# Matrix memory of a hybrid encoder layer: row maxima, sample keys, state decay and score order rewritten, unused products added

## The reference, cut to what matters

```python
def _mlstm_chunk(carry, inp):
    c_mat, n_vec, m_sc = carry
    q, k, v, ig, lf = inp
    b = jnp.cumsum(lf, axis=-1)
    d_log = jnp.where(causal, b[..., :, None] - b[..., None, :] + ig[..., None, :], -jnp.inf)
    g_log = b + m_sc[..., None]
    m_tok = jnp.maximum(g_log, jnp.max(d_log, axis=-1))
    w_intra = jnp.exp(d_log - m_tok[..., None]) * jnp.einsum('bhjd,bhsd->bhjs', q, k)
    inter = jnp.exp(g_log - m_tok)
    num = (inter[..., None] * jnp.einsum('bhvk,bhjk->bhjv', c_mat, q)
           + jnp.einsum('bhjs,bhsv->bhjv', w_intra, v))
    den = inter * jnp.einsum('bhk,bhjk->bhj', n_vec, q) + jnp.sum(w_intra, axis=-1)
    h = num / jnp.maximum(jnp.abs(den), jnp.exp(-m_tok))[..., None]
    m_new = m_tok[..., -1]
    w_state = jnp.exp(b[..., -1:] - b + ig - m_new[..., None])
    decay = jnp.exp(b[..., -1] + m_sc - m_new)
    c_new = decay[..., None, None] * c_mat + jnp.einsum('bhs,bhsv,bhsk->bhvk', w_state, v, k)
    n_new = decay[..., None] * n_vec + jnp.einsum('bhs,bhsk->bhk', w_state, k)
```

## Time and profile before

| | |
|---|---|
| median of 3 runs | 2208.29 us (2206.0 to 2211.57) |
| the profiled execution's own time | 2209.34 us |
| its span (first to last instruction) | 2207.5 us |
| TensorE busy | 2045.0 us, 93% of the span |
| VectorE busy | 1307.6 us, 59% |
| ScalarE busy | 996.7 us, 45% |
| mean granted TensorE clock | 0.938 |

### The profile page before, as it was taken

The page is one execution under the profiler, slowest core; times in us unless marked ns, Lnnn a source line. Parts: engine busy times, 40 slices in busy tenths (PEclk is TensorE's granted clock), DMA queues, the critical chain, the costliest instruction groups (busy, mean ns, idle before and its releaser), DMA issues.

```text
span 2207.5 us, 36654 instructions
## 1 busy us (share of the span) xinstructions
PE 2045.0 (93%) x14269; PEld 1712.1 (78%) x14269; DVE 1307.6 (59%) x2068; ACT 996.7 (45%) x1456; POOL 177.0 (8%) x271
## 2 busy tenths in 40 slices
PE   6999878898999999998999878988899999999996
PEld 4999745588999999998998545876666667788883
DVE  2657654354544544456557553556566667789885
ACT  5522125443433433334321245435455566677782
POOL 3000111110000000000000021111010010010101
PEclk7999768998999999998998589988999999999998
DMA  9222569542645364542213084317677788999995
GB/s 329 69 77 67 156 179 325 173 135 70 174 129 160 124 167 142 160 144 80 77 58 105 13 270 157 133 33 257 225 259 250 257 280 323 332 371 372 376 380 190
DMA packets 272094, 418.21 MB, mean 189 GB/s; under 512 B 21215, under 2 KB 216313, under 8 KB 271953
## 3 DMA queue, kind: packets, MB, share of 16 engines
q1 hardware_dynamic: 249984, 349.50, 48.0%
q0 software_dynamic: 21968, 66.72, 9.3%
HBM read 385.73 MB, written 29.59 MB: 188 GB/s over the span
## 4 chain that ended last, share of the span: by engine, by line
PE 83%; DVE 5%; DMA 4%; ACT 4%; issue 2%; ACTq 0%; POOL 0%; PEldq 0%; DVEq 0%; PEld 0%; SPq 0%; POOLq 0%
PE banks L951 79%; PE banks L955 4%; DMA expert_ring<-in_we 2%; ACT scratch L1900 1%; DVE scratch L2535 1%; DVE region L2535 1%; ACT region_split L1900 1%; DMA scratch<-bias_rows 1%; ACT hidden_t L1900 0%; ACT region L1900 0%; DMA hidden_t<-h_rows,pass_tokens 0%; DVE weights_lower L2535 0%; ACTq L1915 0%; DMA weight_ring<-in_w_ada 0%; DMA region<-in_pool_scale 0%
## 5 line engine op out<-in xcount | busy, mean ns | idle before, releaser
L951 PE MATMUL banks<-upper_parts,region_split 128*128 128x320 f32 x1664 | 391.3, 311 | 4.5 <-DVE upper_parts L2535 4.5
L951 PE MATMUL banks<-upper_parts,weights_lower 128*128 128x320 f32 (+1 forms) x1248 | 387.7, 311 | 0.0
L951 PE MATMUL banks<-region_split 128*128 128x320 f32 (+1 forms) x1264 | 338.9, 331 | 2.8 <-DVE upper_parts L2535 2.8
L2535 DVE TENSOR_TENSOR expert_lower<-expert_ring,region_split 128x1408 fp32r<-128x1408 f32 (+1 forms) x198 | 284.0, 1468 | 87.9 <-PE banks L951 58.1
L951 PEld LDWEIGHTS banks<-upper_parts,region_split 128*128 128x128 f32 x1664 | 285.7, 189 | 4.8 <-issue 4.8
L1900 ACT ACTIVATE region_split<-expert_ring 128x1408 fp32r<-128x1408 f32 (+1 forms) x198 | 242.4, 1257 | 60.9 <-DMA expert_ring<-in_we 60.7
L951 PEld LDWEIGHTS banks<-region_split 128*128 128x128 f32 x1264 | 222.9, 188 | 19.4 <-issue 4.3
L951 PEld LDWEIGHTS banks<-upper_parts,weights_lower 128*128 128x128 f32 (+1 forms) x1248 | 235.8, 189 | 0.0
L951 PE MATMUL banks<-region_split,upper_parts 128*128 128x384 f32 x732 | 226.7, 380 | 0.0
L2535 DVE TENSOR_TENSOR weights_lower<-weight_ring,region_split 128x2048 fp32r<-128x2048 f32 (+2 forms) x72 | 168.9, 2350 | 96.2 <-ACT region_split L1900 96.1
L1900 ACT ACTIVATE region_split<-weight_ring 128x2048 fp32r<-128x2048 f32 (+2 forms) x72 | 140.6, 1958 | 164.2 <-PE banks L951 162.5
(11 more groups left out here) (338 smaller groups left out, 3260.1 us busy)
## 6 DMA issues: line engine op xcount, KB each, us to landing
expert_ring<-in_we SPq DMA_DIRECT2D x176, 704.0 KB, 6.8
expert_ring<-in_we SPq DMA_DIRECT2D x121, 512.0 KB, 4.5
weight_ring<-in_w_ada SPq DMA_DIRECT2D x48, 1024.0 KB, 9.0
weight_ring<-in_w SPq DMA_DIRECT2D x88, 512.0 KB, 5.1
weight_ring<-in_w_in SPq DMA_DIRECT2D x24, 1024.0 KB, 5.2
weight_ring<-in_w SPq DMA_DIRECT2D x16, 1408.0 KB, 6.3
weight_ring<-in_w_out SPq DMA_DIRECT2D x8, 1024.0 KB, 7.0
y_rows<-residual_t POOLq DMA_DIRECT2D x4, 1760.0 KB, 24.2
```

The lines of the kernel that those rows point to most:

```text
L951: return nc.tensor.matmul(out, lhsT, rhs, start=first, stop=last)
L2535: return v.tensor_tensor(out, x, y, op)
```

## The change

Five things, all in the `mlstm` stage but for signs of constants:

1. The row maxima are four products per tile straight from `ML`, with `minus_delta4[:, hd, :]` (4 x 128) as weights; VectorE's `max_rows` and `NMX` are gone.
2. The scores of tile t + 1 are made in tile t, between the products for the state and the wait for `h_ready`.
3. Six unused products per tile: three before the wait for `intra_ready`, three before the wait for `h_ready`.
4. The sample keys are masked by the parity of the sample, for all heads in one VectorE operation (`KWS`, 128 x 512); the products take 32 rows (two samples) each, and bank g then holds two samples for all heads.
5. ScalarE clears and fills `MQM` and decays the samples' states in 32 small activations (8 after t = 2's evictions, 8 in t = 3 ahead of its evictions, 16 after them); VectorE adds the products to the states after it has written `HTM`, behind a new wait `states_decayed`.

```diff
-                def max_rows():
-                    take(max_rows_ready)
+                def max_rows(t, fills=0):
                     claim(0)
-                    hand(mm(PS[:, 0, :], minus_ones[:, :], NMX[:, :, :].rearrange("p h j -> p (h j)"), True, True), "dve", 0)
+                    fill(0, fills)
+                    for hd in range(MH):
+                        ins = mm(PS[:, 0, tiles(hd)], minus_delta4[:, hd, :], sample_tokens(ML) if t == NTP else ML[:, tiles(t)], True, True)
+                    hand(ins, "dve", 0)
+                def memory_scores(t):
                     claim(1, 2)
                     for hd in range(MH):
                         pair, half = divmod(hd, 2)
                         at = slice(half * HD, (half + 1) * HD)
                         ins = mm(PS[:, 1 + half, tiles(pair)], MK[at, pair, tiles(t)], MQ[at, pair, tiles(t)], True, True)
-                        if hd == 0:
-                            free_weights(ins)
+                        free_weights(ins)
                     hand(ins, "dve", 1, 2)
-                max_rows()
+                max_rows(0)
+                memory_scores(0)
                 for t in range(NT):
...
                     if not sample:
                         turn_key_tile(t)
-                        max_rows()
+                        max_rows(t + 1)
                     claim(3)
+                    fill(3, 3)
                     take(intra_ready)
                     for hd in range(MH):
                         ins = mm(PS[:, 3, hd * (HD + 1):(hd + 1) * (HD + 1)], DM[t % 2][:, hd, :], MVA[:, t, hd, :], True, True)
                     hand(ins, "dve", 3)
                     if sample:
-                        for hd, b in enumerate(SAMPLE_BANKS):
-                            claim(b)
-                            take(key_weights_ready)
-                            hand(mm(PS[0:HD + 1, b, :], MVA[:, t, hd, :], KWM[hd % 2][:, :, :].rearrange("p b k -> p (b k)"),
-                                    True, True), "dve", b)
+                        claim(*SAMPLE_BANKS)
+                        take(key_weights_ready)
+                        for hd in range(MH):
+                            for g, b in enumerate(SAMPLE_BANKS):
+                                rows = slice(32 * g, 32 * (g + 1))
+                                ins = mm(PS[0:HD + 1, b, tiles(hd)], MVA[rows, t, hd, :], KWS[rows, hd, :, :].rearrange("p j k -> p (j k)"),
+                                         True, True)
+                                if hd == MH - 1:
+                                    hand(ins, "dve", b)
                     else:
...
                         hand(ins, "dve", 7)
+                        memory_scores(t + 1)
                     claim(6)
+                    fill(6, 3)
                     take(h_ready)
...
+                def decay_states(batches):
+                    for b in batches:
+                        for hd in range(MH):
+                            ins = func(CS[:, b, hd, :], CS[:, b, hd, :], ACT.Identity, scale=DEC[0:HD + 1, hd, NTP + b:NTP + b + 1])
+                    if batches[-1] == NB - 1:
+                        ins.then_inc(states_decayed, 1)
                 decays(0)
+                for pair in range(2):
+                    func(MQM[:, pair, :, :].rearrange("p b t -> p (b t)"), ones[:, 0:1].broadcast_to([P, NB * P]), ACT.Copy, scale=0.0)
+                also(act_link)
+                take(act_link)
+                for pair in range(2):
+                    copy(blocks(MQM, pair), by_batch(MQ[:, pair, SAMPLE]))
+                also(masked_q_ready)
                 for t in range(NT):
                     if t < NTP:
                         decays(t + 1)
+                    if t == NTP - 1:
+                        decay_states((2, 3))
...
+                        decay_states((0, 1))
+                    if t == NTP - 1:
+                        decay_states(range(4, NB))
...
                     if sample:
                         key_weights(t)
-                        keys_by_sample(0)
-                        keys_by_sample(1)
-                        for hd in range(MH):
-                            ins = tt(CS[:, :, hd, :], CS[:, :, hd, :], along(DEC[0:HD + 1, hd, NTP:], 2, HD), ALU.mult)
-                        link(ins)
+                        tt(KWS[:, :, :, :], along(KW[:, :, :], 2, 2), along(along(batch_parity[:, :], 2, HD), 1, MH), ALU.mult)\
+                            .then_inc(key_weights_ready, 1)
                         inter(t)
...
-                    if sample:
-                        for hd, b in enumerate(SAMPLE_BANKS):
-                            take(for_dve)
-                            if hd < 2:
-                                keys_by_sample(hd + 2)
-                            drained(tt(CS[:, :, hd, :], CS[:, :, hd, :], PS[0:HD + 1, b, :].rearrange("p (b k) -> p b k", b=NB),
-                                       ALU.add))
                     tt(HTM[:, :].rearrange("p (h v) -> p h v", h=MH), NUM[:, :, 0:HD],
                        MO[:, t, :].rearrange("p (h v) -> p h v", h=MH), ALU.mult).then_inc(h_ready, 1)
+                    if sample:
+                        take(states_decayed)
+                        for g, b in enumerate(SAMPLE_BANKS):
+                            states = CS[:, 2 * g:2 * g + 2, :, :]
+                            take(for_dve)
+                            drained(tt(states, states, PS[0:HD + 1, b, :].rearrange("p (h j k) -> p j h k", h=MH, j=2), ALU.add))
```

More of the change, by code:

```diff
@@ L337, in build @@
         MQM, CPR, CTP = g(2, NB, P), g(MH, HD, parts=HD + 1), g(2, HD + 1)
-        NMX, DM = g(MH, P, parts=MH), [g(MH, P), tail[3](MH, P)]
+        _, DM = g(MH, P, parts=MH), [g(MH, P), tail[3](MH, P)]
         NUM, T1 = g(MH, HD + 1), g(MH, HD + 1)
@@ L472, in build @@
         intra_logs_ready = sem("intra_logs_ready")
[L473 removed]
+        states_decayed, decays_log_ready, decays_ready = sem("states_decayed"), sem("decays_log_ready"), sem("decays_ready")
         pool_rows_ready = sem("pool_rows_ready")
@@ L1124, in gate_columns @@
                     take(decay_rows_ready)
-                    hand(mm(PS[:, 4, 96:96 + 12 * MH], ones[0:MH, :], DCX[:, :, :].rearrange("p h c -> p (h c)"),
+                    hand(mm(PS[:, 4, 96:96 + 12 * MH], minus_ones[:, :], DCX[:, :, :].rearrange("p h c -> p (h c)"),
                             True, True), "act", 4)
@@ L1223, in _ @@
                 stage(f"z{l}")
-                def max_rows():
-                    take(max_rows_ready)
+                def max_rows(t, fills=0):
                     claim(0)
-                    hand(mm(PS[:, 0, :], minus_ones[:, :], NMX[:, :, :].rearrange("p h j -> p (h j)"), True, True), "dve", 0)
+                    fill(0, fills)
[3 more added lines that the diff above has]
+                def memory_scores(t):
+                    claim(1, 2)
+                    for hd in range(MH):
+                        pair, half = divmod(hd, 2)
+                        at = slice(half * HD, (half + 1) * HD)
+                        ins = mm(PS[:, 1 + half, tiles(pair)], MK[at, pair, tiles(t)], MQ[at, pair, tiles(t)], True, True)
+                        free_weights(ins)
+                    hand(ins, "dve", 1, 2)
                 def turn_key_tile(t):
@@ L2125, in decays @@
                     ins.then_inc(exp_ready, 1)
-                decays(0)
+                def decay_states(batches):
+                    for b in batches:
+                        for hd in range(MH):
+                            ins = func(CS[:, b, hd, :], CS[:, b, hd, :], ACT.Identity, scale=DEC[0:HD + 1, hd, NTP + b:NTP + b + 1])
+                    if batches[-1] == NB - 1:
+                        ins.then_inc(states_decayed, 1)
+                decays(0)
+                for pair in range(2):
[5 more added lines that the diff above has]
+                also(masked_q_ready)
                 for t in range(NT):
@@ L2838, in key_weights @@
                                 along(TOK[:, t, 2, :], 2, HD), ALU.mult, ALU.mult), True)
-                def keys_by_sample(hd):
-                    tt(KWM[hd % 2][:, :, :], along(KW[:, hd, :], 1, NB), along(batch_of[:, :], 2, HD), ALU.mult)\
-                        .then_inc(key_weights_ready, 1)
-                max_rows(0)
                 intra_logs(0)
+                link(v.memset(CPR[:, :, :], 0.0))
                 for t in range(NT):
                     sample = t == NTP
-                    if not sample:
-                        max_rows(t + 1)
-                    if t < 2:
-                        link(v.memset(MQM[:, t, :, :], 0.0))
-                        link(copy(blocks(MQM, t), by_batch(MQ[:, t, SAMPLE])))
-                        if t == 1:
-                            also(masked_q_ready)
                     take(for_dve)
```

34 lines of the change are left out of this document (10 added, 24 removed).

## The result

The changed kernel takes **2185.35 us** (median of 4 runs, 2180.45 to 2189.9) against 2207.87 for the kernel before on the same chip (4 runs): ratio **0.9895 [0.9881, 0.9909]**. I had said 2198, -10 us from the median; it is -22.5. The sign and the range hold, the size does not: the change is over twice what I had. Its profiled execution took 2189.17 us with a span of 2187.5, the mean granted clock is 0.953, and TensorE is busy 2027.0 us, VectorE 1287.7, ScalarE 1016.2.

The account below looks back on a forecast made before the run. In the mlstm stages TensorE at about half clock bounds prompt tiles, VectorE the sample tile. Half-clock sum +0.3 us, full-clock -32.5; a third at full clock gives -10.6, from 2208.3 to 2198 us, range 2184 to 2210.

Parts of the forecast that it names:

- a third of the stage's work at full clock: Both mlstm stages: the share assumed at full clock, the rest at half, giving -10.6 us.
- the head: Start of each mlstm stage to first intra products: -1.5 and -1.2 us at half clock, -1.5 and -2.4 at full.
- E of tile 0: Start of the intra products in the first prompt tile: forecast at 252.4 in layer 0, against 253.90 before.
- J of tile 3: CPR's transpose in prompt tile 3; from first intra products to it, +4.5 us a layer at half clock, -8.8 at full.
- the sample tile: End of each mlstm stage, from the last prompt tile's CPR transpose to the barrier: -3.0 us at half clock, -5.5 at full.
- Rival 1: mlstm stages: the clock rises in part, 2198 us, own range 2190 to 2204; chance 50%.
- rival 3: mlstm stages: clock full nearly throughout, 2176 us, or 2182 with a fifth left at half; chance 12%.
- Rival 2: mlstm stages: clock stays at half, unused products are bare cost, +0.3 us, 2209, range 2205 to 2213; chance 26%.
- Rival 5: Stages after mlstm wait for DMA and give the gain back: 2205 to 2208 us; chance 6%.
- Rival 4: Row maxima: loads don't run under matmuls, 3.4 us instead of 1.85 at half clock, +12.4, 2221 with Rival 2; chance 6%.
- half-clock sum of +0.3: Both mlstm stages at half clock throughout: heads -2.7, prompt tiles 2 x 4.5, sample tiles -2 x 3.0, together +0.3 us.
- ScalarE at no cost: ScalarE's new decays and MQM work in the mlstm stages: costed at nothing, 0.25 us a decay, sixteen taking 4.0 us.

Follow-up runs that it names:

- E4: The changed kernel itself run once more, nothing altered: 2188.01 us, ratio 0.9888 to the kernel before.
- e8: Changed kernel, its three unused products before intra_ready moved to TensorE's idle time between the result's transpose and the next inter products: 2179.55 us, ratio 0.989.
- e3: Changed kernel without the three unused products before the wait for intra_ready, those before h_ready kept: 2187.71 us, ratio 0.9899.
- E1: Changed kernel without its six unused products a tile: 2189.62 us, ratio 0.9909.
- e9: From e8, next tile's row maxima moved ahead of the inter products in place of one unused product, VectorE's mask add moved to match: 2177.59 us, ratio 0.9853.
- e10: As e9, but keeping only the three unused products before the wait for h_ready: 2176.01 us, ratio 0.9842.

## Why the prediction was right in sign and wrong in size

**The step that failed** is "I take a third of the stage's work at full clock": the mechanism was right, and this term was too small. The mean clocks 0.73 and 0.89 are shares at full clock of 2 x 0.73 - 1 = 0.46 and 0.78. With the prediction's own sums the rest follows. Layer 0: half clock -1.5 + 4.5 - 3.0 = 0.0, full -1.5 - 8.8 - 5.5 = -15.8, so -0.46 x 15.8 = **-7.3**; measured 50.27 - 57.76 = **-7.5**. Layer 1: +0.3 and -16.7, so 0.3 - 0.78 x 17.0 = **-13.0**; measured 45.42 - 58.42 = **-13.0**. E4, with 0.72 and 0.81, gives -7.0 and -10.2 by this against -8.4 and -13.0, so the mean clock is good to some 3 us a stage here, and agreement to a tenth is luck.

**What else was mis-sized, and cancelled.** I split a stage as the prediction does: the head up to E of tile 0, the stretch from there to J of tile 3, and the rest, the sample tile. In layer 1, with 0.78 of the full clock, my terms give -2.1, -5.9 and -5.0 and the trace -2.7, -3.8 and -6.5: errors of 2 us that offset each other. The sample tile gained more than I had: from the last J to the barrier is 9.7 us in layer 0, within my 8.4 to 10.9, but 7.4 in layer 1 and 7.0 in e8, below my full-clock 8.4. The end of the sum at full clock has the right size all the same: e8, at 0.92, lies 34.7 below before where the full-clock sum was 32.5.

**Why a third.** The earlier trace rows had stretches at either level and nothing that gave a share between them, so the third was a guess. I had noted the idle stretch behind the scores as the argument against more; that fits e3 and e8, where fills in it raise the clock from 0.68 and 0.70 to 0.92. One reading was wrong, too. I wrote that four wide products are followed by the stretch at 1.00 from 298.0 to 304.5. Before:

```profile
295.13 1.91 PE L951 MATMUL banks<-mix_t,region 128*65 128x512 f32 x2
...
296.83 1.63 PE L951 MATMUL banks<-hidden_t,region 128*65 128x512 f32 x2
...
299.73 1.04 PE L951 MATMUL banks<-mix_t,region 128*65 128x512 f32 x2 [1.27 <-DVE mix_t L2535]
```

Each row is one product of f32. Only two of the four start ahead of the rise at 298.0; the third takes 1.04 us instead of 1.91, so it runs at full clock already.

**Rival 1** was right in kind and too timid; the time fell between it and rival 3. **Rival 2** is refuted by the clocks. **Rival 5** is partly seen in the first layer's prompt attention (+5.0 in one execution, +1.9 in the other), with a cause that is not shown, and takes nowhere near the whole.

**Rival 4** is refuted by two rows: the eight loads and matmuls of the maxima take 2.07 at half clock and 1.15 at full, and start-to-start to the next work 2.01 and 1.09, where loads that don't overlap would take 3.4. I had 1.85 and 1.0, an error of 0.16 a tile. I had taken the rule from the Trainium skill ("TensorE: Matmul & The Clock Gate", section "The mechanism"), whose list says that a load overlaps with matmuls only where their row groups differ; all eight use the same four rows here, and the measurement decides against that line. The sentence ahead of the list allows a second case, a load into the background weight buffer, and with that the trace agrees; I had weighed only the list.

**The tiles.** A half-clock tile was to take 11.3 and took 11.05; a full-clock one 7.4, measured 7.53 (e8, whose fills stand elsewhere). E of tile 0 was to start at 252.4 and started at 252.28.

**What the half-clock sum of +0.3 hid.** It is a large gain less the large cost of the fills. By the prediction's own terms three fills ahead of the intra products cost 1.28 in nine places (three prompt tiles and the sample tile of each layer, and layer 1's head) and three behind the scores 5.05 - 4.12 = 0.93 in eight, 19 us in all. So the rest of the change was to gain about 18.5 at half clock. E1 took the fills out and the stages fell by 17.3 at a clock of 0.54. So my sentence "all hangs on the clock" was wrong in its tone: the structure earned the gain on its own, the fills then paid for themselves and little more. That 18.5 and 17.3 are so near is partly luck. Heads, tile stretch and sample tiles were to gain 3.9, 6.0 and 8.6, and gained 4.2, 2.3 and 10.8: a tile without fills takes 9.56 us where my terms give 9.1, so it is hardly shorter than the 9.83 before, and the fills cost it 1.5 and not 2.2.

**ScalarE at no cost** holds: the sixteen decays in 3.92 us (0.25 each, as taken), done 2.6 us before they are wanted.

## What to carry to other kernels

When an edit does two things, a change of structure and a change of clock, write the sum at both clock levels with the added work as a term of its own; the version without that work (e1) is then the first thing to run, and it may be nearly as good. Unused products pay in time in which TensorE would wait anyway, and where they stand decides what they give: in this kernel three behind the scores plus three in the gap gave a clock of 0.92, three behind the scores and three ahead of the intra products 0.73 and 0.89, three behind the scores alone 0.68 and 0.70, three in the gap alone 0.57 and 0.63. Needed work moved into the gap did at least as well here (e9, e10).

## What the runs showed of the hardware that was not expected

- A stretch in which TensorE is busy 12.77 of 13.50 us, with nine fills in it, can still be granted 0.51 (254.0 to 267.5), while 11.25 of 13.30 with nine fills too was 1.00 in the other layer. The clock of such a stage is not a function of its program alone: the two layers, with the same instructions, had 0.73 and 0.89, and the second layer's stage had 0.89 in one execution and 0.81 in the other. The layers differ in DMA share (0.84 and 0.26); whether that plays a part was not tested.
- Eight weight loads of 4 rows run under the matmuls of the same 4 rows: 2.07 us at half clock, 1.15 at full.
- A higher mean clock is not by itself a shorter stage: the old kernel with fills had 0.83 and 0.81 and took 104.8 us, the new one without fills 0.54 and 98.9.
